# A two-block transformer kernel: output columns added to x in two halves, new layer seams, one load per weight unit, and constant products on TensorE while it waits for x

## The reference

```python
def hybrid_layer(x, ...):            # two layers of it
    p = rms_norm(x, pre_g) @ w_in + b_in      # 6992 columns: sb, nsa, fox, mla, gates
    ...                                       # four attentions; nsa compresses keys with cmp_w1
    mix = concatenate([o_sb * silu(..), o_nsa * silu(..), o_fox * silu(..), o_mla * silu(..)])
    return x + rms_norm(mix @ w_out, post_g)

def second_block(x, ...):
    proj = rms_norm(x, norm1_g) @ w_in        # a (dilated), b (conv), c (window with sinks)
    mix = concatenate([out_a, out_b, out_c])  # 512 + 512 + 1024 columns
    x = x + mix @ w_out
    h2 = rms_norm(x, norm2_g)
    return x + (silu(h2 @ w_gate) * (h2 @ w_up)) @ w_down
```

## Time and profile before

| | us |
|---|---|
| median of 3 runs | 2084.08 (2081.74 to 2085.05) |
| profiled execution, its own time | 2084.3 |
| its span, first to last instruction | 2082.7 |
| PE busy | 2012.2 (97%) |
| DVE busy | 1123.3 (54%) |
| ACT busy | 931.3 (45%) |
| mean granted clock | 0.989 |

### The profile page before, as it was taken

One profiled execution on the slowest core, in us unless ns is written; L12 is line 12 of the kernel. 1 busy time (PEld: TensorE's weight loads), 2 busy tenths in 40 slices (PEclk: granted clock), 3 DMA queues, 4 the chain that ended last, 5 costly groups with the idle time before them and its releaser, 6 DMA issues.

```text
span 2082.7 us, 27966 instructions
## 1 busy us (share of the span) xinstructions
PE 2012.2 (97%) x10370; PEld 1712.6 (82%) x10370; DVE 1123.3 (54%) x1309; ACT 931.3 (45%) x1215; POOL 76.8 (4%) x126
## 2 busy tenths in 40 slices
PE   7999999998999999998999887999999999999998
PEld 6889988887789998887888766888888888888886
DVE  4474555555556464554647864644445544444443
ACT  5355434444454444444554434444444444433442
POOL 3000000001100000001100100000000000000000
PEclk9999999999999999999999999999999999999999
DMA  7584455665665444665545423566666666656553
GB/s 256 163 251 124 137 167 157 186 198 147 201 195 188 140 155 127 206 187 152 169 152 152 129 74 122 181 192 186 189 191 191 191 183 190 191 187 207 202 202 112
DMA packets 209513, 360.80 MB, mean 173 GB/s; under 512 B 22641, under 2 KB 45728, under 8 KB 209152
## 3 DMA queue, kind: packets, MB, share of 16 engines
q1 hardware_dynamic: 203728, 345.36, 54.3%
q0 software_dynamic: 4816, 13.76, 2.3%
q10 hardware_dynamic: 864, 0.27, 0.1%
HBM read 357.23 MB, written 2.10 MB: 173 GB/s over the span
## 4 chain that ended last, share of the span: by engine, by line
PE 90%; DVE 3%; ACT 2%; DMA 1%; issue 1%; SPq 1%; DVEq 1%; ACTq 0%; POOL 0%; POOLq 0%
PE psum L551 24%; PE psum L553 24%; PE psum L552 24%; PE psum L559 3%; PE psum L561 3%; PE psum L562 3%; DVE wl L522 1%; DMA raw<-in_w_in_dram 1%; SPq L506 1%; PE psum L627 1%; DVE conv_y L766 1%; PE psum L867 1%; PE psum L641 1%; PE psum L616 1%; ACT wh L515 1%
## 5 line engine op out<-in xcount | busy, mean ns | idle before, releaser
L522 DVE TENSOR_TENSOR wl<-raw,wh 128x1024 fp32r<-128x1024 f32 (+2 forms) x672 | 797.4, 1197 | 735.9 <-ACT wh L515 728.9
L515 ACT ACTIVATE wh<-raw 128x1024 fp32r<-128x1024 f32 (+2 forms) x672 | 690.5, 1036 | 879.4 <-PE psum L553 712.1
L551 PE MATMUL psum<-wh,xh 128*128 128x512 f32 (+2 forms) x1600 | 623.7, 390 | 1.2 <-DVE xl L809 1.2
L553 PE MATMUL psum<-wh,xl 128*128 128x512 f32 (+2 forms) x1600 | 616.7, 385 | 0.0
L552 PE MATMUL psum<-wl,xh 128*128 128x512 f32 (+2 forms) x1600 | 616.5, 385 | 0.0
L551 PEld LDWEIGHTS psum<-wh,xh 128*128 128x128 f32 x1600 | 302.3, 189 | 62.6 <-DVE xl L809 2.9
L553 PEld LDWEIGHTS psum<-wh,xl 128*128 128x128 f32 x1600 | 301.9, 189 | 59.5
L552 PEld LDWEIGHTS psum<-wl,xh 128*128 128x128 f32 x1600 | 302.6, 189 | 57.4
L551 PE MATMUL psum<-wh,mh 128*128 128x512 f32 x384 | 153.3, 399 | 18.0 <-issue 9.8
L553 PE MATMUL psum<-wh,ml 128*128 128x512 f32 x384 | 152.2, 396 | 0.0
L552 PE MATMUL psum<-wl,mh 128*128 128x512 f32 x384 | 152.0, 396 | 0.0
(11 more groups left out here) (342 smaller groups left out, 1509.7 us busy)
## 6 DMA issues: line engine op xcount, KB each, us to landing
raw<-in_w_in_dram SPq DMA_DIRECT2D x264, 512.0 KB, 4.3
raw<-in_w_out_dram SPq DMA_DIRECT2D x96, 512.0 KB, 3.7
raw<-in_w_gate_dram SPq DMA_DIRECT2D x88, 512.0 KB, 3.6
raw<-in_w_up_dram SPq DMA_DIRECT2D x88, 512.0 KB, 3.6
raw<-in_w_down_dram SPq DMA_DIRECT2D x80, 512.0 KB, 4.1
bias<-in_b_in_dram POOLq DMA_DIRECT2D x18, 256.0 KB, 4.0
raw<-in_w_in_dram SPq DMA_DIRECT2D x16, 268.0 KB, 2.8
raw<-in_nsa_cmp_w_k_dram SPq DMA_DIRECT2D x32, 128.0 KB, 2.3
```

Source lines behind the costliest of these rows:

```text
L515: act.activation(wh[:, n % SPLIT_SLOTS, 0:k, 0:unit.n], raw[:, n % RAW_SLOTS, 0:k, 0:unit.n], ACT.Copy).then_inc(hi_done, 1)
L522: dve.tensor_tensor(out=wl[:, n % SPLIT_SLOTS, 0:k, 0:unit.n], in0=raw[:, n % RAW_SLOTS, 0:k, 0:unit.n], in1=wh[:, n % SPLIT_SLOTS, 0:k, 0 ...
L551: pe.matmul(o, ah_[:, kt, tok], hi_w, start=first, stop=False)
L553: ins = pe.matmul(o, al_[:, kt, tok], hi_w, start=False, stop=last)
```

## The change

It touches only host-side layout, the order of work and the waits; the large products stay the same in number. The cores of the diff, in the order of the file:

```diff
+SMALL_COLUMNS = ((3072, 268), (5388, 4), (6416, 64))   # w_small: packed on the host, 336 columns
+        source, pieces = ("w_small", ((0, N_SMALL),)) if name == "nsa_win_small" else (weight, pieces)
-    units = [Unit("cmp_w1", tuple((c, HD) for c in range(0, 4 * HD, HD)), (2 * j, 2 * j + 1), "cmp", None, "cmp",
+    units = [Unit("cmp_w1", ((0, 4 * HD),), (2 * j, 2 * j + 1), "cmp", None, "cmp",
 def output_slots():
+    units[-1].by_rows = True       # multiply: all of rows tb 0, then tb 1; tb 0 signals "first_rows"
 def output_slots_2():
+    # early(g, ...): pairs 4..7 of group g as a sum of its own; late(g, ...): pairs 0..3
+    slots = [early(0, 4, 5), early(1, 4, 5), early(0, 6, 7) + early(1, 6), early(1, 7), early(2, 4, 5, 6),
+             early(2, 7), early(3, 4), early(3, 5, 6, 7) + late(0, 0, 1), late(0, 2, 3) + late(1, 0, 1),
+             late(1, 2, 3), late(2, 0, 1, 2, 3), late(3, 0, 1), late(3, 2, 3)]
+    slots[7][3].after_mid = 22
+    slots[8][0].after = "conv_rows2"
+    slots[8][2].after_mid = 23
+CONV_UNIT = sum(len(s) for s in SLOTS_2[:WIN_SLOTS_2 + 8]) + 1
 def pe_turn_block(name, updates, b):
+            if b == 0 and updates:
+                nc.tensor.wait_ge(s("x_half"), updates)
...
+                if b == 0 and updates and i == 0:
+                    wait_x(nc.tensor, name, updates, b)
 def act_first(place, name, updates, scratch, units):
             if updates:
+                act_operand(place, name, 0)
+                act_operand(place, name, 1)
...
+                ahead = n + 1 if updates else n     # units 0 to 2 were split in next_splits
 def dve_first(place, name, updates, units, update, last_group):   # updates > 0
+            update(0); operand(0); operand(1); update(1); split(3); last_group(); operand(2); operand(3)
+            update(2); split(4); split(5); operand(4); operand(5); update(3); split(6); operand(6); split(7); operand(7)
+        def pe_idle_products(n, wide=True):
+            for _ in range(n):
+                if wide:
+                    nc.tensor.matmul(acc[0][:, 0, 0:384].rearrange("p (a c) -> p a c", a=3), ident_b[:, :],
+                                     over(causal_b[:, :], 3), start=True, stop=True, skip_group_check=True)
+                else:
+                    nc.tensor.matmul(acc[0][:, 0, 0:P], ident[:, :], ident[:, :], start=True, stop=True, ...)
 def pe_first_operand(place, name, n, updates):
-                for b in {0: (0, 1), 2: (2,), 5: (3,)}.get(n, ()):
+                if n == 0:
+                    pe_idle_products(*((18, True) if updates else (14, False)))
+                for b in {0: (0,), 1: (1,), 3: (2,), 5: (3,)}.get(n, ()):
                     pe_turn_block(name, updates, b)
+                if n == 0:
+                    pe_idle_products(*((8, True) if updates else (12, False)))
 SP:
-                        if l == 0 and n < BLOCKS:
-                            load_x(n)
+                        if l == 0 and n in (0, 2, 3, 4):
+                            load_x(max(n - 1, 0))
                         load_unit(sp, place, n, unit, layer_src(l))
+                        if l == 0 and n == PARTS - 1:   # the 8 constants that ACT's queue issued
 POOL:
+            pool.wait_ge(x_loaded[BLOCKS - 1], 16)      # before its 7 constants
-                pool_rstd(place.once, "post", [(slice(0, TB), DM)])
+                pool.tensor_tensor(out=rstd[:, 0:TB], in0=sq_sums[:, 0:TB], ..., op=ALU.pow)
 PE stages of block 2:
-                2: lambda: turn_pairs(cqn, 0), ... 28: lambda: turn_final_x(range(8, EARLY_KT)),
+                3: lambda: turn_pairs(cqn, 0), ... 27: lambda: turn_final_x(range(8, EARLY_KT)),
 ACT:
+                def ahead_of_last():                # before mid 35
+                    next_splits(l)                  # splits of the next layer's units 0 to 2, DVE too
+                    act.wait_ge(s("first_rows"), place.once)
+                    output_squares(3, [0])
-                    35: lambda: output_squares(3),
+                    35: lambda: output_squares(3, [1]),
 def conv_rstd():
+                act.activation(sink_e[:, 0:1], eps, ACT.Silu)
+            after_unit[CONV_UNIT] = lambda: (conv_silu(), act.drain(), conv_high())   # was mid 23
-                12: lambda: act_copy_half(probT2),          # 14 and 18 alike
+                12: lambda: act_copy_all(probT2),
 DVE:
 def update(b):      # block 0 in two halves of 256 columns, the first signals "x_half"
+                def mean_of_three_groups():     # in mid 33; close_layer adds group 3 in one instruction
-            taps_at_unit = {... enumerate((4, 4, 3, 3, 3)) ...}
-            taps_at_mid = {9: 2, 15: 3, 16: 4, 17: 2, 18: 3}
+            taps_at_unit = {... enumerate((4, 2, 3, 3, 3)) ...}     # and one behind each unit of slots 16, 17
+            taps_at_mid = {9: 2, 15: 1, 16: 4, 18: 5}
+            after_unit[CONV_UNIT] = conv_low
-                1: first_queries (with head_scale "cq02"), 3: kv_group,
+                1: first_queries, 2: lambda: head_scale("cq02", 0, 512, split_heads(cqn)), 3: kv_group,
-                11: lambda: (head_sums("aq2", 512), sinks_max("c10", 8), head_scale("aq2", ...), sinks_sum("c10")),
-                12: lambda: (dve_copy_half(probT2)),
+                11: lambda: (sinks_max("c10", 8), head_sums("aq2", 512), sinks_sum("c10")),
+                12: lambda: head_scale("aq2", 1, 512, split_heads(aqn)),        # 13 and 14 in the same way
-                22: lambda: (conv_sumsq(), dve_mix_low(...)), 23: conv_low,
-                24: lambda: add_output(0), 25: lambda: add_output(1), 26: lambda: final_x_low(range(0, 8), 1),
-                27: lambda: add_output(2), 28: lambda: final_x_low(range(8, EARLY_KT), 2), 29: last_output,
+                18: lambda: add_output(0),
+                19: lambda: (softmax_max("a4"), small_out(o_a, 0), softmax_sum("a4"), add_output(1)),
+                22: lambda: (conv_sumsq(), add_output(2), dve_mix_low(place, "a", mh2, ml2, 0, 0)),
+                23: lambda: add_output(3),
+                24: lambda: add_output(0), 25: lambda: add_output(1),
+                26: lambda: (add_output(2), final_x_low(range(0, 8), 1)),
+                27: lambda: final_x_low(range(8, EARLY_KT), 2), 28: last_output,
```

More of the change, by code:

```diff
@@ L63 @@
 OPERAND_ALIGN = 2048
+SMALL_COLUMNS = ((3072, 268), (5388, 4), (6416, 64))
+N_SMALL = sum(w for _, w in SMALL_COLUMNS)
 GROUPS = (
@@ L111, in input_units, with unit @@
 def input_units(weight, groups):
[L113 to L114 removed]
+    def unit(name, pieces, g, layout, j):
+        source, pieces = ("w_small", ((0, N_SMALL),)) if name == "nsa_win_small" else (weight, pieces)
+        return Unit(source, pieces, (2 * j, 2 * j + 1), layout, g % 2, "x", KT, j == 0, j == KT // 2 - 1)
+    return [unit(name, pieces, g, layout, j) for g, (name, pieces, layout) in enumerate(groups)
+            for j in range(KT // 2)]
 def output_unit(weight, g, pair, last_pair, first_pair=0):
@@ L134, in output_slots, with early, late @@
     units[6].after_mid = NG * 2
+    units[-1].by_rows = True
     return slots_of(units)
 def output_slots_2():
[L141 to L150, removed]
+    def early(g, *pairs):
+        return [output_unit("w_out_2", g, pair, 7, 4) for pair in pairs]
+    def late(g, *pairs):
+        return [output_unit("w_out_2", g, pair, 3, 0) for pair in pairs]
+    slots = [early(0, 4, 5), early(1, 4, 5), early(0, 6, 7) + early(1, 6), early(1, 7), early(2, 4, 5, 6),
[4 more added lines that the diff above has]
+    slots[8][2].after_mid = 23
+    return slots
 CMP_SLOTS = (6, 7)
@@ L530, in multiply @@
                 pe.wait_ge(dve_mid_done, place.slots + unit.after_mid + 2)
+            if unit.after is not None:
+                pe.wait_ge(s(unit.after), 1)
             pe.wait_ge(lo_done, RAW_SLOTS + place.units + n + 1)
@@ L542, in multiply @@
             out_ = acc[unit.pair]
+            if unit.by_rows:
+                for tb in range(TB):
+                    tok = slice(tb * P, (tb + 1) * P)
+                    for kk, kt in enumerate(unit.kts):
+                        o, hi_w, lo_w = out_[:, tb, 0:unit.n], wh[:, slot, kk, 0:unit.n], wl[:, slot, kk, 0:unit.n]
+                        pe.matmul(o, ah_[:, kt, tok], hi_w, start=False, stop=False)
+                        pe.matmul(o, ah_[:, kt, tok], lo_w, start=False, stop=False)
+                        ins = pe.matmul(o, al_[:, kt, tok], hi_w, start=False, stop=kk == len(unit.kts) - 1)
+                    ins.then_inc(s("first_rows") if tb == 0 else unit_used, 1)
+                return
             for kk, kt in enumerate(unit.kts):
@@ L1418, in slots_with_mids, with next_splits @@
                 act_mid(place, len(slots) - 1, n, mids.get(len(slots) - 1, nothing))
+            def next_splits(l):
+                layer_follows = l + 1 < LAYERS
+                place = in_layer(l + 1) if layer_follows else after(0, 0)
```

(9 more changed lines are left out.)

156 lines of the change are left out of this document (94 added, 62 removed).

## The result

The changed kernel takes 2049.5 us (median of 4 runs, 2047.95 to 2053.95) against 2084.6 (4 runs beside it, 2081.74 to 2085.68): a ratio of 0.984, 95% interval 0.982 to 0.986. The forecast was 2050, range 2038 to 2065. The profiled execution took 2047.95 with a span of 2046.3, which is 36.4 less than the 2082.7 of before; the sum had forecast 34.1. The profile is of the fastest of the 4 runs; the medians differ by 35.1. The total agrees better than the terms do.

What follows compares the result with a forecast made beforehand. PE, busy 97%, was taken as the bound: its work, 70.5 us idle and lower-clock loss. Gains 1.1 + 7.9 + 4.2 + 2.3 + 6.7 + 11.9 = 34.1 off 2084.3 gave 2050, range 2038 to 2065.

Steps and rivals of the forecast that it cites:

- term 2: Loads of slots 6 and 7, both layers: fewer transfers with longer rows leave 1.0 us idle of 8.95; gain 7.9.
- term 5: Slot 12 of block 2: DVE work moved from ahead of the softmax maximum shortens PE's wait, clock returns; gain 6.7.
- The start: Kernel start: block 0 turned alone, constant products, earlier second weight; unit 1 done at 18.9 instead of 20.0; gain 1.1.
- the seams: Both seams: first product 5.7 us after the last instead of 9.2, unit 6 at 25.4; gain 4.2 in all.
- stage 2 of block 2: The turn of cqn, one slot later, no longer waits 2.3 us for POOL's power and DVE's scaling; gain 2.3.
- term 6: Slots 16 to 24 of block 2: idle 12.4 us instead of 19.95, plus 4.4 of clock; gain 11.9.
- rival D: Loads of slots 6 and 7 stay half bound, 4 of 8.95 us remain: 2053; chance within the forecast's 0.50.
- rival B: Clock isn't held behind seams and waits: seams give 1.1 less, slot 12 and slots 16 to 24 some 6: 2057; 0.14.
- Rival E: Slots 16 to 24: DVE is not late anywhere, 12 us idle fall to 4 and the clock stays: 2039; chance 0.16.
- A: Short slots from 1201.4 on serialise PE and DVE, idle up to 58.5 us: 2101, slower; chance 0.04.
- F: Nothing moves: the waits pass to the load path or to DVE in sum: 2083; chance 0.03.

Runs made afterwards that it cites:

- e10: Changed kernel with the bias of nsa_win_small in one transfer into its own tile, loaded at the layer's start: 2044.9 us, ratio 0.9808.
- e12: Changed kernel with e10's early bias but the old loads of slots 6 and 7 (three and four transfers a unit): 2050.8 us, ratio 0.9848.
- e2: Changed kernel without the constant products at the start and the two seams: 2057.35 us, ratio 0.9865.
- e6: Changed kernel with e4's bias, group 1's late units first in slot 24 and add_output(3) behind the convolution's normalising: 2043.4 us, ratio 0.98.
- e8: Changed kernel with e4's single bias transfer, constant products kept at the seams, none at the start: 2047.2 us, ratio 0.9819.
- e9: The repeat: the changed kernel once more, unedited, beside e8: 2051.8 us, ratio 0.9839.
- e1: Changed kernel with the old loads of slots 6 and 7 (three and four transfers a unit): 2051.1 us, ratio 0.9841.
- e4: Changed kernel with the bias of nsa_win_small packed on the host and loaded in one transfer instead of three: 2044.5 us, ratio 0.9816.
- e5: Changed kernel with the packed bias of nsa_win_small in three transfers of 112 columns: 2051.3 us, ratio 0.9842.
- e7: Changed kernel with e4's bias and the row scaling of av moved from DVE's mid 15 to ACT: 2043.2 us, ratio 0.9802.
- e11: Changed kernel with e10's early bias, e6's order and e7's scaling together: 2038.1 us, ratio 0.9778.

## Why the prediction was right, and where it was not

The forecast of 2050 holds, because terms that were off by up to 4.3 us cancelled: term 2 gave 4.3 us less than forecast and term 5 gave 1.2 less. The start gave 1.0 more, the seams 1.4, stage 2 of block 2 1.4 and term 6 3.65, and 0.45 came in a stretch that I had at nothing. That the total came so near is partly luck. The two bounds in the sum are slightly off as well: every lower bound gives 2075 and every upper one 2032, not 2074 and 2034.

*1, the start: right.* 1.0 us by the turn of block 3, 1.1 forecast; unit 0 starts at 12.7, forecast 12.5. The repeat turns block 3 1.4 us earlier, so the start scatters by more than this term. I had not counted a wait at stage 2 of layer 1 that shrank by 1.1.

*2, the loads: the step that failed,* mis-sized at 7.9. It measured 3.6 in one profile, below my lower bound of 4.5, and nothing in the other. The step is "I leave 1.0 idle", which was reckoned from the rate of SP's transfers and a landing of some 3.5 us. The sums over stages 2 to 8 of both layers, before, changed kernel and repeat (length of the stretches, then each engine's busy time):

```profile
sum 170.89, PE 161.94 PEld 137.88 DVE 95.17 ACT 75.42 POOL 6.08; mean PE 80.97 PEld 68.94 DVE 47.59 ACT 37.71 POOL 3.04
sum 167.34, PE 162.61 PEld 139.54 DVE 95.56 ACT 77.16 POOL 6.38; mean PE 81.30 PEld 69.77 DVE 47.78 ACT 38.58 POOL 3.19
sum 171.49, PE 164.65 PEld 141.98 DVE 97.01 ACT 79.55 POOL 7.33; mean PE 82.33 PEld 70.99 DVE 48.51 ACT 39.77 POOL 3.67
```

PE's idle time, the length less its busy time, went from 8.95 to 4.7, and to 6.8 in the repeat, where I had 1.0. Its busy time rose, by 0.7 and 2.7, because the clock fell behind single waits of 2.3 to 3.5 us (mean clock of the stretches 1.00 in both layers before, 0.98 and 1.00 in the changed kernel, 0.98 and 0.96 in the repeat); the term had no such loss. The landings measured 4.2 us at best and 5.3 to 7.5 beside POOL's three bias broadcasts. Those were in no line of the working, though the row of 100 to 126 in the earlier trace rows shows them (POOL, 1.59, x3). e10 shows them as the cause: with them out of the way the stretches take 162.5 instead of 170.9, 8.4 less. But that isn't the loads' 7.9 come true. The early bias alone gives 2.0 with the old loads (e12, 168.9), so the new loads give 6.4 beside it, and beside the three broadcasts 1.8, the mean of five profiles (169.2) against 171.0. This is rival D by its size (4 of 8.95 stay idle); of its two reasons, rule or round trip, it is the round trip, and that POOL's transfers lengthen it was not in it.

On the rate itself, e12 and e10 have a pair in which only the loads' rows and number differ: 264 GB/s at a share of 0.90 with pieces of 16 to 1072 B, 290 at 0.91 with rows of 1.3 and 2 KB. By the Trainium skill ("DMA: Bandwidth & Descriptors", Specifications) the compress rows of 512 B were at line rate already; these runs changed them together with the tiny pieces, so what the 512 B rows cost alone is not shown.

*3, the seams: right in sum, wrong in its parts.* First product at 5.7 and unit 6 at 25.3, as reckoned. By the turn of block 3 it is 5.6, and 0.9 of it is given back before unit 6, where DVE's chain is late by 0.3 twice. What was mis-sized is the part of the constants: rival B has it at 1.1 for the seams, and e2 gives it as 4.6, all of it clock. The earlier first product, which I took for the main source of the gain, gives 1.0 without them.

*4, stage 2 of block 2: wait right, size 1.4 short.* The wait of 2.3 went whole. The 1.4 beside it is products at a lower clock behind the wait (0.21 us apart instead of 0.12, the clock 0.77 from 1019 to 1025 before and 1.00 in the changed kernel), which I had looked for only at the larger waits.

*5, slot 12: 5.5 for 6.7.* The wait is 1.1, forecast 0.9. What stood at 0.52 behind it was mostly transposes (2.79 us then, 1.50 now), so 1.2 came back and not 1.9, and 0.3 us of a new wait for a split followed.

*6, slots 16 to 24: 15.55 for 11.9.* PE's idle time between stage 15 and the FFN fell from 20.0 to 9.4, by 10.6, forecast 7.5; its busy time fell by 4.9, forecast 4.4. The 4.9 is in part luck: 3.0 us of loss were forecast for two waits of 3 us, and in this profile only the convolution's cost anything. In the repeat both did, and the term is 13.9. The waits that the walk held for large were right, and stage 27's too: 2.9 at slot 18 (2.9 forecast), 3.2 for the convolution (3.0), 1.1 at stage 27 (1.1). The small ones were too many: 1.4 at slots 16 and 17 didn't come, stage 20 had 0.6 of 1.6. Rival E said this and was right for these mids, not for the three large ones.

SiLU's table load is followed by its function at once here as well (load of 1.28 us at 1255.20, function at 1256.49, and the instruction ahead of the load ends at 1255.11), so the drain that the Trainium skill has ("ScalarE: Activation LUTs", What ACT_TABLE_LOAD costs) does not show in this trace. A did not happen: the stretch of 82.9 us has 8.0 idle, far from the 42 at which it decides. F did not either.

## What to carry to other kernels

Before a set of loads is made faster, look at what the other queues transfer in the same microseconds: here three small broadcasts of POOL's took back most of what larger rows had won, and neither edit paid much without the other. Price constant products in a wait by what the clock costs behind it: here they gave 4.6 us at two seams, and at the start, where they hold unit 0 back by 2.0 us, no gain that can be told. And compare a forecast term by term: this one hit the total within 2.3 us of span while its second term was off by 4.3.

## What the hardware showed that I had not expected

Waits of the same length at the same place lower the clock in one execution and not in the next: 2.89 us at slot 18 without a loss, 2.83 with eight products at 0.43 us apart. Ten profiles have slot 18's wait at 2.8 to 2.9 us: six of them (e2, e6, e8, e9, e10, e12) go on with six to eight products at 0.43 us, four (the changed kernel, e1, e4, e5) don't. The convolution's wait of 2.8 to 3.2 lowers the clock in six of ten as well. Cut to 1.4 to 1.7 us (e6, e7, e11), neither wait did. One such loss costs some 1.5 us: from stage 15 to the last turn of x PE is busy 125.2 us in e4 and e5, with none, and 126.8 in the changed kernel, with one. A kernel with several waits of about 3 us scatters by some us in part for that reason, in part by the loads of slots 6 and 7 (2047.95 to 2053.95 here; e11, without either, 2037.5 to 2040.1). What decides between the two outcomes stays open.

The granted-clock column is no witness at the very start. In e8's first unit the products are 0.43 us apart, and the row of that stretch says 1.00:

```profile
10.70:15.80 5.10, 5.08 (x13) 4.01 (x14) 3.02 (x4) 1.35 (x2) 0.00 (x0) 1.00 1.05 408
```

The trace's first record of the clock in e8 begins only at 15.40; ahead of it the column reads 1.00 without one, so there the distance between products has to be read.
